# Attention work of the forgetting and the dilated heads in two slots a tile instead of three

## What is computed

```python
def forgetting_attention(q, k, v, log_f):          # per head, 128 queries at a time
    c = jnp.cumsum(log_f, axis=-1)
    logits = einsum(qb, k) * scale + (cb[..., :, None] - c[..., None, :])
    logits = jnp.where(kpos <= qpos, logits, -1e30)
    p = jax.nn.softmax(logits, axis=-1)
    return einsum(p, v)

def _dilated_group(q, k, v, table_g, dilation, span):
    s = einsum(qb, kk) * (DIL_HEAD_DIM ** -0.5) + bias
    p = jnp.exp(s - max(s)); den = jnp.sum(p)
    o = einsum(p, vv) / den
```

## Time and profile before

| | |
|---|---|
| median of 3 runs | 3191.28 us (3190.74 to 3192.82) |
| profiled execution, time | 3190.43 us |
| profiled execution, span | 3188.6 us |
| PE busy | 3149.9 us, 99% |
| DVE busy | 1525.3 us, 48% |
| ACT busy | 1106.9 us, 35% |
| POOL busy | 255.7 us, 8% |

### The profile page before, as it was taken

How to read it: one execution, slowest core, us unless ns; L and a number is a source line. 1 busy time by engine, 2 the same in 40 slices (tenths; PEclk the granted TensorE clock), 3 DMA queues, 4 the chain that set the end, 5 groups by cost and what they waited for, 6 DMA issues and landing times.

```text
span 3188.6 us, 36988 instructions
## 1 busy us (share of the span) xinstructions
PE 3149.9 (99%) x14924; PEld 2572.2 (81%) x14924; DVE 1525.3 (48%) x2374; ACT 1106.9 (35%) x1564; POOL 255.7 (8%) x230
## 2 busy tenths in 40 slices
PE   8999999999999999999999999999999999999998
PEld 6888887788888888888877788888888777788887
DVE  5434435455443444344455555434656444464352
ACT  4323335333322333223344333222456433332222
POOL 1000104002000010000030021000200000110001
PEclk9999999999999999999999999999999999999999
DMA  4322322222423232233222233332322332322322
GB/s 134 99 94 95 125 88 72 69 75 96 136 96 99 90 103 95 97 99 109 88 71 73 66 100 106 99 96 89 120 90 85 98 109 88 96 94 99 99 93 73
DMA packets 91550, 303.08 MB, mean 95 GB/s; under 512 B 10228, under 2 KB 16500, under 8 KB 90832
## 3 DMA queue, kind: packets, MB, share of 16 engines
q1 hardware_dynamic: 91380, 300.71, 29.2%
HBM read 298.52 MB, written 5.29 MB: 95 GB/s over the span
## 4 chain that ended last, share of the span: by engine, by line
PE 96%; issue 2%; DVE 1%; ACT 1%; POOL 0%; DMA 0%; SPq 0%; POOLq 0%; DVEq 0%; ACTq 0%
PE bank L1570 89%; PE score_ps L1416 1%; PE out_ps L1449 1%; PE turn_ps L1427 1%; PE out_ps L1468 1%; PE score_ps L1458 1%; PE score_ps L1490 1%; PE turn_ps L1385 1%; PE turn_ps L1436 0%; PE turn_ps L1337 0%; ACT w_hi L1598 0%; PE out_ps L1502 0%; DVE tmp L2089 0%; PE score_ps L1533 0%; DMA xT<-x_in 0%
## 5 line engine op out<-in xcount | busy, mean ns | idle before, releaser
L1972 DVE TENSOR_TENSOR w_lo<-raw,w_hi 128x1024 fp32r<-128x1024 f32 (+1 forms) x548 | 677.3, 1237 | 1256.5 <-ACT w_hi L1598 1255.2
L1570 PE MATMUL bank<-in_hi,w_hi 128*128 128x512 f32 x2704 | 1080.9, 400 | 18.9 <-DVE in_lo L1978 12.0
L1570 PE MATMUL bank<-in_hi,w_lo 128*128 128x512 f32 x2704 | 1054.9, 390 | 0.0
L1570 PE MATMUL bank<-in_lo,w_hi 128*128 128x512 f32 x2704 | 1053.7, 390 | 0.0
L1598 ACT ACTIVATE w_hi<-raw 128x1024 fp32r<-128x1024 f32 (+1 forms) x548 | 568.2, 1038 | 1134.8 <-PE bank L1570 1129.0
L1570 PEld LDWEIGHTS bank<-in_hi,w_hi 128*128 128x128 f32 x2704 | 508.4, 188 | 148.2 <-issue 32.6
L1570 PEld LDWEIGHTS bank<-in_hi,w_lo 128*128 128x128 f32 x2704 | 507.8, 188 | 108.6
L1570 PEld LDWEIGHTS bank<-in_lo,w_hi 128*128 128x128 f32 x2704 | 508.6, 188 | 102.6 <-issue 2.4
L1570 PE MATMUL bank<-hid_hi,w_hi 128*128 128x512 f32 x960 | 373.4, 389 | 0.0
L1570 PE MATMUL bank<-hid_lo,w_hi 128*128 128x512 f32 x960 | 373.4, 389 | 0.0
L1570 PE MATMUL bank<-hid_hi,w_lo 128*128 128x512 f32 x960 | 373.4, 389 | 0.0
(11 more groups left out here) (331 smaller groups left out, 2755.4 us busy)
## 6 DMA issues: line engine op xcount, KB each, us to landing
raw<-w_ffn_in SPq DMA_DIRECT2D x176, 512.0 KB, 3.3
raw<-w_mix SPq DMA_DIRECT2D x90, 512.0 KB, 3.4
raw<-w_ffn_out SPq DMA_DIRECT2D x80, 512.0 KB, 3.4
raw<-w_mixb SPq DMA_DIRECT2D x58, 512.0 KB, 3.4
raw<-w_mlp_in SPq DMA_DIRECT2D x32, 512.0 KB, 3.3
raw<-w_mlp_out SPq DMA_DIRECT2D x32, 512.0 KB, 3.3
raw<-w_w_out SPq DMA_DIRECT2D x16, 512.0 KB, 3.3
raw<-w_ffn_out SPq DMA_DIRECT2D x16, 256.0 KB, 2.8
```

Source lines behind the costliest of these rows:

```text
L1570: mm = pe.matmul(ps, lhs, rhs, start=first and step == 0, stop=last and step == 2, skip_group_check=True)
L1972: dve.tensor_tensor(w_lo[:, i % SPLIT, 0:cols], raw[:, i % RAW, 0:cols], w_hi[:, i % SPLIT, 0:cols].bitcast(F32), ALU.subtract).then_inc(S ...
```

## The change

A forgetting tile takes two slots. Slot A holds the turn of head 0 of the tile before and the scores of this one. Slot B holds the values of two tiles before, the turn of head 1 of the tile before, the mask of the next tile, and behind these `fox_exp` and now also `fox_scale` of this tile. A dilated tile also takes two slots: the values of two tiles before (every second tile), the 4-block turn of the tile before, and the scores; then the 2-block turn. The empty slots at the start of the forgetting queue go. The rate of the forgetting and first retention units goes from 2.75 to 2.1, and that of the dilated units from 1.9 to 1.3.

```diff
     def fox_exp(self, s):
         s["exp"] = [self.add("exp") for k in range(2)]
         self.item("fox_exp", s=s)
-        self.lagged.append(lambda: self.fox_scale(s))
+        self.fox_scale(s)
...
         for n in range(pair_tiles + 2):
-            if n < pair_tiles:
-                self.filler.append(lambda n=n: self.fox_scores(n))
-
-            def values_and_turn(n=n):
+            def first_turn_and_scores(n=n):
+                if 0 <= n - 1 < pair_tiles:
+                    self.fox_turn(n - 1, 0)
+                if n < pair_tiles:
+                    self.fox_scores(n)
+
+            def values_and_second_turn(n=n):
                 if n >= 2:
                     self.fox_values(n - 2)
-                if 0 <= n - 1 < pair_tiles:
-                    self.fox_turn(n - 1, 0)
-
-            def second_turn(n=n):
                 if 0 <= n - 1 < pair_tiles:
                     self.fox_turn(n - 1, 1)
                 if n + 1 < pair_tiles and n % TT != TT - 1:
                     self.fox_mask(n + 1)
-            self.filler.extend([values_and_turn, second_turn])
+            if n <= pair_tiles:
+                self.filler.append(first_turn_and_scores)
+            self.filler.append(values_and_second_turn)
...
-        self.rate = 2.75
+        self.rate = 2.1
...
         for n in range(GH * DIL + 2):
-            def values_and_scores(n=n):
+            def values_turn_and_scores(n=n):
                 if n >= 2 and n % 2:
                     self.dil_values(n - 2)
+                if 0 <= n - 1 < GH * DIL:
+                    self.dil_turn(n - 1, 0, 4)
                 if n < GH * DIL:
                     self.dil_scores(n)
-            self.filler.append(values_and_scores)
+            self.filler.append(values_turn_and_scores)
             if 0 <= n - 1 < GH * DIL:
-                self.filler.append(lambda n=n: self.dil_turn(n - 1, 0, 4))
                 self.filler.append(lambda n=n: self.dil_turn(n - 1, 4 * P, 2))
-        self.rate = 1.9
+        self.rate = 1.3
...
-            self.rate = 1.9
+            self.rate = 1.3
```

## The result

The changed kernel takes 3203.64 us (median of 6 runs, 3202.34 to 3205.56) against 3191.65 for the kernel before in the same session (6 runs, 3190.74 to 3193.54). The recorded ratio is 1.0035, 95% interval 1.0025 to 1.0046 (the two medians by themselves give 1.0038). By the medians that is slower by 12.0 us, where 8.9 had been forecast, and inside the range. The profiled execution took 3203.74 us with a span of 3201.9. Its span is 13.3 us longer than the profiled span before, 3188.6.

The account below looks back on a forecast made before the run. PE, busy for 99% of the span, was taken to set the end. The terms -0.6 + 8.0 - 1.1 + 2.6 = +8.9 us on 3190.43 gave 3199.3; with the median 0.85 higher, 3200, range 3191.5 to 3209.

Parts of the forecast that it names:

- Forgetting waits, +8.0: Forgetting heads: turns wait for late scaled probabilities in 14 tiles, 3.5 us in layer 0 and 4.5 in layer 1.
- Rival 1: Forgetting heads: short waits are covered, only the long ones stand; +4.8 us, 3196; chance 0.25.
- Decay waits, -1.1: Forgetting heads: waits of the second decay matmul go, its distance growing from two steps to three or more; -1.1 us.
- Merges, -0.6: Slot boundaries: 45 turns lose their own slot, -1.4 us; seven dilated slots with a turn between cost +0.8.
- Rival 2: Slot boundaries: each of the 45 merges saves 0.11 us, -5.0 in all, giving 3195.8; chance 0.10.
- Dilated, +2.6: Dilated heads: changed waits for scaling, copies and banks; +2.6 us in sum, bounds 0.5 and 5.
- tile 0: First dilated tile: the next slot begins with a turn that waits for the scaling; +1.15 us.
- the first values: Dilated heads, unit 439: values wait longer for a 2-block copy on ACT; +0.9 us, bounds 0 and 1.8.
- unit 444: Dilated heads: the bank is freed later, with the softmax of tile 5 directly ahead; +0.7 us.
- 455 and 458: Dilated heads: bank waits shrink from 2.1 us to 1.3 at each unit; -1.6 us together.
- 461: Dilated heads: this unit waits for its bank because unit 460 now holds a turn; +1.3 us.
- Rival 3: Waits spread: units start late, 0.5 us more for each of some 20 slots, 3210; chance 0.10.

Follow-up runs that it names:

- exp_first: The whole change, but a tile's exponentials and scaling issued at the head of slot B, ahead of values and turn; 3196.48 us, ratio 1.0012.
- rate2: The whole change with the rate of the forgetting units 2.0 instead of 2.1; 3198.77 us, ratio 1.0016.
- fox_rate2: Kernel before with only the forgetting heads on two slots, at rate 2.0, dilated slots standing as before; 3192.02 us, ratio 0.9998.
- fox_only: Kernel before with only the forgetting heads on two slots a tile, at rate 2.1, dilated heads keeping three; 3212.65 us, ratio 1.0059.
- before_again: The kernel before, unchanged, measured and profiled once more; 3193.15 us, ratio 0.9999.
- dil_gap3: Only the dilated half, its slots placed as in the changed kernel, plus one empty slot ahead of tile 3's first; 3198.45 us, ratio 1.0017.
- dil_only: Kernel before with only the dilated heads on two slots a tile, at rate 1.3, forgetting heads keeping three; 3198.92 us, ratio 1.0020.

## Why the prediction was right, point by point

- **Forgetting waits, +8.0.** In the profile both layers grew by 6.8, and the decay waits that went are 1.1: 7.9 us of waits. The tables above give 8.05 in the 14 tiles that were named, and none is off by more than 0.07. exp_first shows that they hang on the exponentials' place on ACT, and rate2 that they hang on the phase of the slots. Rival 1 (the short waits vanish) would have left about 4 and fell. On the ports shared by VectorE and GpSimd, the rule of the Trainium skill ("SBUF — State Buffer", Who interferes with whom) allowed tile 5 of layer 1 some 0.9 us beyond the sum. The trace agrees, and shows why no wait beyond the sum came. The turn started 0.2 us after the end of the GpSimd product that was under way (1644.30), and the second scaling ended 0.14 us after the end of the next one (1645.58). The first product had 0.61 us left when the first scaling began, and not a whole one.
- **Decay waits, -1.1.** Gone, as the list shows.
- **Merges, -0.6.** This term was wrong. Behind a slot the second projection matmul starts 0.32 us after the first in place of 0.23, so a boundary does cost 0.09. But a merged slot is longer than its parts: a 4-block turn with forgetting scores takes 0.95 (rate2), apart 0.36 and 0.51 (before). The one cancels the other, and 30 merges gave 0.1 us in fox_rate2. The prediction read the boundary and did not look inside the slot. Rival 2, at 0.11 each, fell. In seven dilated slots the turn between values and scores costs more, as below.
- **Dilated, +2.6.** The waits were right. By distances of starts, exp_first against before, tile 0 grew by 1.28 (1.15 forecast), the first values by 0.93 (0.9), unit 444 by 0.80 (0.7), 455 and 458 by -1.8 together (-1.6), and 461 by 1.27 (1.3). The 0.15 at unit 452 did not come. That makes 2.5. But without the clock the part cost 3.9 (exp_first). The merges account for 0.9 more: seven slots of values, turn and scores take 3.19 where the parts took 2.60 and 0.36, eight of turn and scores 1.58 where they took 0.36 and 1.14, less 0.09 for each of 15 boundaries. About 0.5 stays open.
- **What was left out: the clock.** It accounts for 1.1 us in the untouched part and for 1.6 behind the first values (5.4 against exp_first's 3.9). 6.8 + 3.9 + 2.7 = 13.4 is the profile's 13.3. The forecast of 8.9 lacked the 2.7 and was 1.8 low on the rest: 1.4 at the merges (+0.8 in place of -0.6) and the 0.5 that stays open, while the waits came within 0.2. How much of the 2.7 a given execution has is chance, and so is part of how near the median came to the forecast. The profiled execution of before happened to be one without any stretch. The median hides part of this, since other executions of before have the stretches too: its runs spread over 5 us, and in the last session those with a mean granted clock of 0.998 lie at 3190.4 to 3191.7, those with 0.996 at 3193.2 and above.
- **Rival 3** (unit starts late) did not come. No bank wait stands in the forgetting parts.

The carried credit of the planner, which the prediction took into its slot tables without a word, turned out to be the largest single number of the study. With the slots as in before it costs nothing, and it costs 12.4 us in fox_only.

## What to carry to other kernels

When slots of side work are merged, look at the distance from each producer's last step to its consumer's new slot, on every engine between. The saved boundary is worth nothing here, because the merged slot is longer by as much, and every wait is paid in full when PE is 99% busy. Compare the length of a merged slot with its parts, and not the boundary alone. A planner that carries a fractional credit makes one region's rate change the next region's order, so set the credit at the start of each region before two halves of a change are compared. A slot layout is worth as much as its worst neighbours: one slot moved removed 5 us at one place and cost more than 6 at another. Before small differences are explained, profile the unchanged kernel twice.

## What the runs showed of the hardware

- PE's granted clock fell to 1.2 GHz for 3.4 us or twice that. In the dilated part it fell within a wait or up to 1.5 us behind it (waits of 1.81 and 3.14 us in fox_only, 2.03 in before_again, 2.46 in after, 2.90 in dil_gap3). A single stretch cost 1.1 to 1.6 us, a double one in the untouched part 2.5 to 2.7. Such waits also passed without one: 1.8 in dil_only, 2.0 in before, 2.46 in exp_first, and the second one of 2.92 in dil_gap3. At the wait of 3.7 us near the end of the program it fell in all 14 profiles. What decides was not tried.
- At 2289 us, ahead of the memory heads, the listed waits are 1.1, 0.7 and 0.2 us in before's two profiles alike. One of them ran at full clock, the other had 6.8 us at half. So no long wait is needed ahead of a fall.
- A wait list can be low by what the pipe drains: 0.15 and 0.17 us at the two long waits here, and all of the shortest.
- Beside GpSimd products of 1.3 us, two VectorE scalings of 256 columns ended 0.2 us or less behind the end of a product each, 2.03 us for both where 0.61 is usual.
- From the start of ACT's split to PE's restart at the next bank it was 3.55 or 3.56 us in the kernels before, after and dil_gap3, whatever stood ahead of it.
